# Recurrence inverse: the doubling rounds on 32 of 64 columns

## What is computed

```python
def rwkv7_scan(r, w, k, v, kk, bb, s0, reverse):
    def step(s, inp):
        r_t, w_t, k_t, v_t, kk_t, b_t = inp
        sa = jnp.einsum('bhij,bhj->bhi', s, kk_t)
        s = s * w_t[:, :, None, :] - sa[..., None] * b_t[:, :, None, :] + v_t[..., None] * k_t[:, :, None, :]
        return s, jnp.einsum('bhij,bhj->bhi', s, r_t)
    xs = tuple(jnp.moveaxis(t, 1, 0) for t in (r, w, k, v, kk, bb))
    s, ys = lax.scan(step, s0, xs, reverse=reverse)
    return s, jnp.moveaxis(ys, 0, 1)
```

## Time and profile before

| what | value |
|---|---|
| median of the runs | 3060.09 us |
| the profiled execution | 3051.25 us |
| its span (first to last instruction) | 3049.4 us |
| PE busy | 2768.1 us (91%) |
| DVE busy | 1873.5 us (61%) |
| ACT busy | 1167.6 us (38%) |
| POOL busy | 1027.6 us (34%) |
| passes of the recurrence (2024 to 2494 us) | 470 us, 12 passes |

### The profile page before, as it was taken

How to read it: one execution, slowest core, us unless ns; L and a number is a source line. 1 busy time by engine, 2 the same in 40 slices (tenths; PEclk the granted TensorE clock), 3 DMA queues, 4 the chain that set the end, 5 groups by cost and what they waited for, 6 DMA issues and landing times. The chain is left out here.

```text
span 3049.4 us, 59055 instructions
## 1 busy us (share of the span) xinstructions
PE 2768.1 (91%) x24960; PEld 2191.1 (72%) x24960; DVE 1873.5 (61%) x2795; ACT 1167.6 (38%) x2168; POOL 1027.6 (34%) x576
## 2 busy tenths in 40 slices
PE   7998898999989988989999799978888887799987
PEld 5775576878867655767788587857777775579875
DVE  5998656887059996478860555547777744363062
ACT  4634434333246344243331422235444533332252
POOL 1432142545424311324454122235555530033202
PEclk9999999999999999999999899989999988899988
DMA  6331133433333211244333332320000004142211
GB/s 226 91 84 49 43 90 99 145 118 94 100 86 101 71 44 50 83 130 147 114 96 95 101 106 88 97 66 19 25 24 24 25 9 152 35 118 77 66 29 56
DMA packets 350230, 249.36 MB, mean 82 GB/s; under 512 B 10874, under 2 KB 322448, under 8 KB 349456
## 3 DMA queue, kind: packets, MB, share of 16 engines
q1 hardware_dynamic: 342704, 229.56, 25.0%
q10 hardware_dynamic: 7264, 16.03, 1.7%
HBM read 221.52 MB, written 16.52 MB: 78 GB/s over the span
## 5 line engine op out<-in xcount | busy, mean ns | idle before, releaser
L545 POOL TENSOR_TENSOR weights_lo<-weights_raw,weights_hi 128x1024 fp32r<-128x1024 f32 (+1 forms) x214 | 546.5, 2555 | 1008.9 <-ACT weights_hi L514 1008.9
L1188 PE MATMUL psum<-moving_hi,weights_hi 128*128 128x512 f32 x1344 | 542.6, 404 | 34.7 <-PEq L173 13.7
L1188 PE MATMUL psum<-moving_lo,weights_hi 128*128 128x512 f32 x1344 | 530.0, 394 | 0.0
L1188 PE MATMUL psum<-moving_hi,weights_lo 128*128 128x512 f32 x1344 | 529.4, 394 | 0.0
L1188 PEld LDWEIGHTS psum<-moving_hi,weights_hi 128*128 128x128 f32 x1344 | 255.8, 190 | 143.1 <-issue 60.0
L514 ACT ACTIVATE weights_hi<-weights_raw 128x1024 fp32r<-128x1024 f32 (+1 forms) x218 | 226.3, 1038 | 227.5 <-PE psum L1188 227.5
L1188 PEld LDWEIGHTS psum<-moving_hi,weights_lo 128*128 128x128 f32 x1344 | 256.0, 190 | 55.2
L1188 PEld LDWEIGHTS psum<-moving_lo,weights_hi 128*128 128x128 f32 x1344 | 256.6, 191 | 47.7
L2630 POOL TENSOR_TENSOR second_off<-second_mats,second_masks 128x256 f32<-128x256 f32 x180 | 150.1, 839 | 108.6 <-PE psum L2087 107.7
L545 POOL TENSOR_TENSOR odd_lo<-odd_raw,odd_hi 128x2048 fp32r<-128x2048 f32 x16 | 74.4, 4649 | 318.8 <-ACT odd_hi L514 318.8
L2686 PE MATMUL psum<-hn_hi,even_hi 128*128 128x256 f32 x480 | 166.1, 346 | 7.3 <-DVE hn_lo L2023 7.3
(11 more groups left out here) (473 smaller groups left out, 6430.3 us busy)
## 6 DMA issues: line engine op xcount, KB each, us to landing
weights_raw<-in_w_up SPq DMA_DIRECT2D x88, 512.0 KB, 3.7
weights_raw<-in_w_in SPq DMA_DIRECT2D x80, 512.0 KB, 3.6
ada<-in_ada_w SPq DMA_DIRECT2D x9, 2048.0 KB, 8.9
odd_raw<-in_od_w_in SPq DMA_DIRECT2D x16, 1024.0 KB, 5.6
even_raw<-in_ev_w_in SPq DMA_DIRECT2D x30, 512.0 KB, 4.0
weights_raw<-in_w_down SPq DMA_DIRECT2D x32, 448.0 KB, 3.6
weights_raw<-in_w_o SPq DMA_DIRECT2D x16, 512.0 KB, 3.9
weights_raw<-in_w_down SPq DMA_DIRECT2D x16, 512.0 KB, 3.8
```

The costliest lines, as they stand in the source:

```text
L545: ops.tensor_tensor(self.ring.lo[i % n][:, a:b], self.ring.raw[:, t % self.ring.landing, a:b], self.ring.hi[i % n][:, a:b].bitcast(F32), A ...
L1188: return nc.tensor.matmul(to, (hi, lo)[which][:, at:at + P], moving(k)[part], start=start and k == 0 and i == 0, stop=stop and k == n_k - ...
```

## The change

At a level with blocks of l, the product Y = `off` x W is zero in half of W's columns, because `off` has only the blocks beside the diagonal and W is triangular within its blocks. The change leaves these columns out. PE multiplies only the 32 columns of `wb` that lie in the right blocks (every second run of l columns, read with a stride), Y and W stand packed in PSUM with 32 columns a chunk, ACT copies 32 columns a chunk, and DVE adds 32 columns a chunk, with a stride in `wb`. At the last level Y is still taken whole, and only the W product is halved. The stationary operands keep their 64 columns everywhere. The masks on POOL, the transposes on DVE, the waits and the order of instructions stay.

```diff
-            bank_y, bank_w = lambda n: bank(n % 2, CH), lambda n: bank(2 + n % 2, CH)
+            half = CH // 2
+            bank_y = lambda n, level: bank(n % 2, half if level < last_level else CH)
+            bank_w = lambda n: bank(2 + n % 2, half)
+
+            def blocks(x, level, odd):
+
+                return x.rearrange("p c (b two l) -> p c b two l", two=2, l=LEVELS[level])[:, :, :, odd, :]
+
+            def y_at(g, level):
+                return y[:, own(g), 0:half if level < last_level else CH]
...
+                            begun = buf.wb[:, slots(g), CH:]
+                            begun = blocks(begun, level, d) if level < last_level else begun
                             for c in range(4):
-                                last = halves_matmul(nc, bank_y(n)[:, c, :], off[:, n % 2, c, :], buf.wb[:, slots(g).start + c, CH:])
+                                last = halves_matmul(nc, bank_y(n, level)[:, c, :], off[:, n % 2, c, :], begun[:, c])
...
-                                wt, y_ = buf.wb[:, s0 + c, 0:CH], y[:, own(g).start + c, :]
-                                last = halves_matmul(nc, bank_w(n)[:, c, :], *((wt, y_) if level < last_level else (y_, wt)))
+                                wt, y_ = buf.wb[:, s0 + c, 0:CH], y_at(g, level)[:, c, :]
+                                if level == last_level:
+                                    wt, y_ = y_, wt[:, half * (1 - d):half * (1 - d) + half]
+                                last = halves_matmul(nc, bank_w(n)[:, c, :], wt, y_)
...
-                            S.activation(y[:, own(g), :], bank_y(n), ACT.Identity).then_inc(y_taken, 1)
+                            S.activation(y_at(g, level), bank_y(n, level), ACT.Identity).then_inc(y_taken, 1)
...
-                            w_ = buf.wb[:, slots(g), CH:] if level < last_level else buf.wb[:, slots(g), 0:CH]
-                            V.tensor_tensor(w_, w_, bank_w(n), ALU.add).then_inc(w_added, 1)
+                            if level < last_level:
+                                w_ = blocks(buf.wb[:, slots(g), CH:], level, d)
+                            else:
+                                w_ = blocks(buf.wb[:, slots(g), 0:CH], level, 1 - d)
+                            made = bank_w(n).rearrange("p c (b l) -> p c b l", l=LEVELS[level])
+                            V.tensor_tensor(w_, w_, made, ALU.add).then_inc(w_added, 1)
```

## The result

| | before | after |
|---|---|---|
| median of 10 runs each, us | 3058.69 (3055.33 to 3067.09) | 3073.05 (3054.20 to 3086.24) |
| profiled execution, us | 3051.25 | 3072.78 |
| its span, us | 3049.4 | 3070.9 |
| its mean granted clock | 0.960 | 0.946 |

The ratio is 1.0038, with a 95% interval of 1.0022 to 1.0055: the changed kernel is slower, by about 12 us, and above my range (3073.05 us, or 3070.3 by the ratio, against at most 3066). The runs of the changed kernel also lie further apart, and their time goes with their mean granted clock: 3054.20 us at 0.955, 3063.21 at 0.951, 3073.32 at 0.946, 3086.24 at 0.940.

What follows compares the result with a forecast made beforehand. PE's own rate was taken to bound the rounds. Gains of 0 us on TensorE, 9.2 us through ACT and DVE and 0 us for strides gave 3060.09 - 9.2 = 3050.9 us, range 3038 to 3066 us.

Steps and rivals of the forecast that it cites:

- rival C: TensorE's clock falls in the passes as narrowed groups carry less work: a third of every pass, 3107 us; chance 0.08.
- rival B: Moving columns set the pace of the rounds' products, so halving them shortens each group: 3007 us; chance 0.12.
- TensorE's own rate: Y and W products in the rounds: the load of 64 stationary columns paces each step, so 0 us gain.
- ACT and DVE: Shorter copies and additions in the rounds, 102 and 132 ns each, shorten PE's waits for the steps: 9.2 us gain.
- five waits: PE's weight loads waiting for the steps' copies, state, copy of Y and outputs on ACT and DVE: 39.0 us before.
- rival A2: PE's waits only move, set by the steps' serial chain: 0 to 3 us gain, about 3058 us; chance 0.09.
- Strided reads and writes: PE's and DVE's strided operands in the rounds cost 0 us; at four times the read price, 15 us for level 0.
- Rival D: Strided operands cost more than the gain: 9.2 us less, 15 us more, 3066 us; chance 0.03.
- What would show it: Signs in the changed kernel's trace: loads 0.55 us, copy near 280 ns, addition near 266 ns, shorter waits, clock 1.00.

Runs made afterwards that it cites:

- the kernel with wide products: Changed kernel with all round products moving 64 columns again, ACT copying and DVE adding only 32: 3047.75 us, ratio 0.9969 to the kernel before.
- the kernel without the stride: Changed kernel with Y products below the last level reading the first 32 columns in one run (wrong values): 3078.75 us, ratio 1.0078 to the kernel before.
- split product: Each round product split in two of 32 stationary columns: on the changed kernel 3177.94 us; with 64 moving columns, ACT and DVE at 32, 3176.00 us.

## Why the prediction was wrong

The step that failed is TensorE's clock. The sum had no term for it, which puts it at 0 us; the clock stood only in rival C, with a chance of 0.08 and outside the range. The runs show 21 to 24 us lost by it. The gain on ACT and DVE came, and was smaller than this loss.

**TensorE's own rate: right.** The 16 loads still span 0.55 us, so the term is near 0 us, and rival B is out. The Trainium skill, "TensorE: Matmul & The Clock Gate", section "LDWEIGHTS", has a load take its number of columns over 1.2 GHz; by that figure I estimate 0.053 us for 64 and 0.027 us for 32. The traces have both 0.006 us longer: 0.059 us a step with 64 stationary columns, 0.033 us with 32.

**ACT and DVE: right in size, with some luck.** I had 102 ns for a copy and it was 107; I had 132 ns for an addition and it was 128. I expected 9.2 us in all, and the kernel that has this part alone gains 9.7, by its interval 6 to 13. From 2024 us to the end of the rounds its five waits sum to 29.8 us, against 39.0. But the earlier trace rows leaves out the longest wait of the same view, the one for nothing that the profile shows. Here it is, first before and then in the kernel with wide products:

```profile
PEld psum L2087 <- issue: 31.9, 33, 7.1
...
PEld psum L2087 <- issue: 34.8, 36, 7.3
```

It grew by 2.9 us, a third of what the five waits lost, and ten passes are 5.9 us shorter (399.4 to 393.5), 0.6 us each and not 0.7 to 0.8. The two profiled executions lie 6.7 us apart. So rival A2 holds in part, some of the waits moved; as the whole story, with 0 to 3 us gained, it is out. "The waits of PE that are left belong mostly to the steps" was wrong as well: the five are 39 us, and the other waits of that view add up to more than 70.

**Strided reads and writes: right.** The strided addition takes 270 ns, where 266 were expected of a contiguous one, the loads of a Y product span 0.54 us at level 0 and 0.55 at level 3, and the kernel without the stride is no faster. Rival D is out.

**Rival C: this is the step that failed.** I had the mechanism and gave it 0.08. The prediction put it so: "a pass carries 982 - 216 = 766 records' worth, 21 a us, against 11 in the stretch that lost the clock. That is nearer to the old passes, hence the low chance." Two things were wrong with it. The first is the mean over a pass, which hides the stretches that it is made of: level 0 has 24 records a us where the pass has 27. If half the columns of its 3 Y and 3 W groups (96 records) go, it is left with (158 - 48) / 6.8 = 16 records' worth a us in the changed kernel (158 are its records from 2070.80 to 2077.60), nearer to 11 than to the old 27. Levels 0 and 1 are where the runs put the cause. This count alone would not have told it either: by the same working level 1 keeps (166 - 48) / 5.4 = 22 a us and level 3, where narrow products cost less, (144 - 48) / 5.0 = 19. The second is the reference: one stretch at 11 that lost the clock and passes at 27 that kept it leave the whole space between open, and "nearer to the old passes" was a guess about where in it the edge lies.

The price was mis-sized too, the other way. I had taken a third of every pass's rounds as lost, 56 us, and 3107 us in all. The twelve passes had 80 us at the half level, but that is not all lost: ten passes of the changed kernel (the second to the eleventh) take 417.1 us together against 393.5 us in the kernel with wide products, 23.6 us more for the 75 us of the half level that lie in these ten, or 0.3 us for each. A product's 0.47 us becomes 0.86, but DVE's and ACT's serial chains beside it, and PE's waits for them, do not double; that this is why the price is 0.3 and not 0.5 us for each is my reading, not a test. The balance is -9.7 us from the engines and some 21 to 24 us from the clock, which makes +11 to +14 us, as measured; the second term is worked out from these same times and is no check of its own.

**The range** reached up to 3066 us, by rival D, and left out both C and B. The profile had one row that speaks of the clock, and a change that takes work from a paced engine without making it faster moves it towards that row. The clock rival should have had more chance than B, whose own term I had argued to be 0.

**What would show it.** That list told the case apart at once: loads at 0.55 us, copy and addition as forecast, the waits for L2187, L2190 and L2199 down by 6.3 us, and the one sign for C, a clock under 1.00 between 2040 and 2490 us.

What stays open is why the Y products cost more than the W products, and what lowers the clock: the runs show that fewer moving columns at levels 0 and 1 lose it, at the same number of instructions and of loads, and no more.

## What to carry to other kernels

When a matmul's stationary load paces it, cutting its moving columns saves little or nothing; skip the zeros on the engines that read and write the results, and leave the matmul wide. Work that looks free to remove can be what keeps TensorE at its full clock, as it was here: before removing it, look at each stretch that it touches, the one with the most waits first, not at the mean of the stage; and test the narrow form in one stretch at a time. And where PE's busy time grows after its work has shrunk, read the granted clock first.

## What the runs showed beyond this

With 32 moving columns a split product's loads span 0.34 us where a whole one's span 0.55 (0.49 us with 64), but the kernel is 4% slower at either moving width, and for the wide one the clock of a pass is not to blame:

```profile
2164.00:2214.00 50.00, 41.53 (x1523) 32.58 (x1522) 25.01 (x57) 18.29 (x60) 21.03 (x23) 0.97 0.12 36
```

1523 records where a pass had 1052 to 1060, in 50 us for 39. The split adds 240 matmuls to a pass, 2880 in all, and costs 121 us, some 42 ns for each added matmul, which includes the waits in which PE waits for nothing that the profile shows. It looks as if PE were short of instructions to start; this was not tested. Nor was the other thing that the split adds tested: products of 32 stationary columns that take turns with the steps' products of 64.
